# Hybrid encoder layer on one core: four places for the out projection's weight tiles, the residual stream loaded in pieces, and a quarter of the second half's new stream made by GpSimd

## The reference

```
xn   = rms_norm(h); P = xn @ w_in                    # q, k, v, gate_b, gate_c, conv_in
attn = stick-breaking attention over 8 heads         # exp(log_sigmoid(z) + reverse cumsum)
conv = gate_b * causal_conv3(gate_c * conv_in)
mix  = group_rms_norm(concat(attn, conv))
h    = h + rms_norm(mix @ w_out)                     # the out projection; "the new stream"
xf   = rms_norm(h)
ff   = silu(xf @ w_gate) * (xf @ w_up)               # 2048 -> 5632
h    = h + rms_norm(ff @ w_down)                     # 5632 -> 2048
```

## Time and profile before

| | us |
|---|---|
| median of 3 runs (2458.87 to 2461.89) | 2460.73 |
| the profiled execution | 2464.63 |
| its span | 2462.9 |
| TensorE busy | 2377.5 (97%) |
| VectorE busy | 1588.0 (64%) |
| ScalarE busy | 1052.2 (43%) |
| GpSimd busy | 95.9 (4%) |
| DMA, mean | 141 GB/s |

### The profile page before, as it was taken

The page is one execution under the profiler, slowest core; times in us unless marked ns, Lnnn a source line. Parts: engine busy times, 40 slices in busy tenths (PEclk is TensorE's granted clock), DMA queues, the critical chain, the costliest instruction groups (busy, mean ns, idle before and its releaser), DMA issues.

```text
span 2462.9 us, 42442 instructions
## 1 busy us (share of the span) xinstructions
PE 2377.5 (97%) x18250; PEld 2334.8 (95%) x18250; DVE 1588.0 (64%) x1852; ACT 1052.2 (43%) x1306; POOL 95.9 (4%) x158
## 2 busy tenths in 40 slices
PE   8999999999997988699999999999999989999998
PEld 7999999999997987599999999999999989999998
DVE  5323333343434556877877787777777778888886
ACT  6345444433233344444444444444444333333346
POOL 0000000000011111000000000000000000000002
PEclk9999999999998998899999999999999999999999
DMA  7222322232325565344444435344544766654562
GB/s 235 83 74 73 94 76 83 70 92 80 87 86 178 163 176 149 108 135 135 159 143 140 149 131 166 123 162 135 167 135 155 262 203 229 230 164 143 173 203 86
DMA packets 365406, 346.82 MB, mean 141 GB/s; under 512 B 9084, under 2 KB 323860, under 8 KB 365092
## 3 DMA queue, kind: packets, MB, share of 16 engines
q1 hardware_dynamic: 334528, 289.99, 37.8%
q10 hardware_dynamic: 30692, 54.12, 6.1%
HBM read 283.08 MB, written 61.00 MB: 140 GB/s over the span
## 4 chain that ended last, share of the span: by engine, by line
PE 84%; DMA 7%; DVE 5%; ACT 3%; issue 1%; SPq 0%; ACTq 0%; POOLq 0%; POOL 0%; DVEq 0%
PE ps L1033 36%; PE ps L449 23%; PE ps L1092 16%; DMA w_raw<-in_w_out_dram 5%; PE ps L750 4%; PE ps L694 2%; PE ps L949 2%; DVE w_lo L435 1%; ACT w_hi L429 1%; DMA ff_lo_scr<-hid_lo 1%; DMA panel<-in_w_down_dram 1%; DVE xs L1894 1%; DVE t_lo L1943 0%; DVE panel L1959 0%; PE ps L1014 0%
## 5 line engine op out<-in xcount | busy, mean ns | idle before, releaser
L1033 PE MATMUL ps<-xs,t_hi 128*128 128x272 f32 x4864 | 923.0, 289 | 23.6 <-DVE xs L1894 19.4
L1033 PEld LDWEIGHTS ps<-xs,t_hi 128*128 128x128 f32 x4864 | 766.3, 189 | 24.8 <-issue 24.8
L1033 PE MATMUL ps<-xs,t_lo 128*128 128x272 f32 x2432 | 704.8, 290 | 0.0
L1943 DVE TENSOR_TENSOR t_lo<-panel,t_hi 128x1024 fp32r<-128x1024 f32 (+1 forms) x402 | 482.0, 1199 | 221.9 <-ACT t_hi L1453 218.8
L1453 ACT CAST t_hi<-panel 128x1024 fp32r<-128x1024 f32 (+1 forms) x402 | 410.3, 1021 | 445.6 <-PE ps L1092 222.3
L1092 PE MATMUL ps<-xd,t_hi 128*128 128x272 f32 x2464 | 468.3, 289 | 9.9 <-DVE t_lo L1943 5.0
L1033 PEld LDWEIGHTS ps<-xs,t_lo 128*128 128x128 f32 x2432 | 458.6, 189 | 0.0
L1092 PEld LDWEIGHTS ps<-xd,t_hi 128*128 128x128 f32 x2464 | 388.6, 189 | 11.6 <-issue 6.3
L1092 PE MATMUL ps<-xd,t_lo 128*128 128x272 f32 x1232 | 357.1, 290 | 0.0
L435 DVE TENSOR_TENSOR w_lo<-w_raw,w_hi 128x1024 fp32r<-128x1024 f32 x162 | 198.1, 1224 | 239.8 <-ACT w_hi L429 239.6
L449 PE MATMUL ps<-act_hi,w_hi 128*128 128x280 f32 (+1 forms) x1536 | 328.8, 295 | 2.1 <-DVE act_lo L1719 1.9
(11 more groups left out here) (203 smaller groups left out, 2200.4 us busy)
## 6 DMA issues: line engine op xcount, KB each, us to landing
w_raw<-in_w_in_dram SPq DMA_DIRECT2D x96, 512.0 KB, 3.8
panel<-in_w_up_dram SPq DMA_DIRECT2D x44, 1024.0 KB, 5.4
panel<-in_w_gate_dram SPq DMA_DIRECT2D x43, 1024.0 KB, 5.1
w_raw<-in_w_out_dram SPq DMA_DIRECT2D x64, 512.0 KB, 4.0
panel<-in_w_down_dram SPq DMA_DIRECT2D x32, 1024.0 KB, 6.1
ff_hi_scr<-hid_hi SPq DMA_DIRECT2D x22, 952.0 KB, 4.5
ff_lo_scr<-hid_lo SPq DMA_DIRECT2D x22, 952.0 KB, 7.4
xd<-ff_hi_scr ACTq DMA_DIRECT2D x28, 544.0 KB, 7.8
```

What stands on the lines that cost most here:

```text
L1033: mm = nc.tensor.matmul(out, w[:, k, :], xs[x][:, part, k, :], start=begins and k == 0 and w is hi and part == 0, stop=k == KH - 1 and w i ...
L1943: V.tensor_tensor(tile_of(t_lo, i), raw_tile(i), tile_of(t_hi, i).bitcast(F32), ALU.subtract)\
```

## The change

It does five things.

1. From out tile 8 on (`WIDER`), tiles with k % 4 of 2 and 3 go to a second pair of places, `raw_more`, in the room of panel 0. Tile t from 12 on waits for tile t - 4 instead of t - 2. The first panel of step 0 now waits until all 68 tiles are subtracted, as the second did.
2. The stream is loaded in four pieces of four chunks, each behind one of the tile groups 2 to 5. VectorE waits for all four before its first addition, no longer before its first scaling.
3. In the last round (e = 31) neither ScalarE nor VectorE treats a tile; those tiles come behind it. The logarithm's table is loaded at the head of rounds 15 and 31, not between the roundings and the square.
4. Scaling and addition of the last four chunks of half 1 are GpSimd's. ScalarE waits for `pool_made` before it squares them. The combine T4 of step 0 and the split of the ring tiles T3 and T1 of step 0 stand ahead of the second row scale, no longer in step 0.
5. In step 46 (`LAST + 3`) the second panel is issued ahead of the wait for the last hidden activations and their stores, and five of the reloads of hidden activations come one step later.

```diff
+        raw_more = sb_at("raw_more", 121856, [P, 2 * TK * P])
+        WIDER = 8
+        def out_tile(phase, k):
+            return 4 * phase[1] + k if phase[0] == 4 else -1
-        def raw_slot(k):
+        def raw_slot(phase, k):
+            if out_tile(phase, k) >= WIDER and k % 4 >= 2:
+                return raw_more[:, (k % 2) * TK * P:(k % 2 + 1) * TK * P]
             return w_raw[:, (k % 2) * TK * P:(k % 2 + 1) * TK * P]
+        def raw_loaded(phase, k):
+            o = out_tile(phase, k)
+            if o >= WIDER:
+                in_place = (o - WIDER) // 4 + 1
+                if k % 4 >= 2:
+                    return out_loaded[k % 2], 16 * in_place
+                return w_loaded[k % 2], 16 * (loads_of((4, WIDER // 4, T_OUT), k % 2 - 2) + in_place)
+            return w_loaded[k % 2], 16 * loads_of(phase, k)
...
@@ load, on SP
-                if not known(t) or t >= 2:
+                o = out_tile(phase, k)
+                if o >= WIDER + 4:
+                    sp.wait_ge(lo_ready, t - 3)
+                elif o >= WIDER + 2:
+                    sp.wait_ge(n1_ready, HEADS + GROUPS)
+                elif not known(t) or t >= 2:
                     sp.wait_ge(lo_ready, t - 1)
...
-            sp.dma_start(resid, h_scr).then_inc(h_loaded, 16)
             for q in range(2, KC):
                 load_out(q)
+                if q < 6:
+                    c0 = 4 * (q - 2)
+                    sp.dma_start(resid[:, c0:c0 + 4, :], h_scr[:, c0:c0 + 4, :]).then_inc(h_loaded, 16)
...
-            sp.wait_ge(n1_ready, HEADS + GROUPS)
+            sp.wait_ge(lo_ready, T_FF)
             load_panel(0, 0)
-            sp.wait_ge(lo_ready, T_FF)
             load_panel(0, 1)
...
@@ the loop over steps, on SP
+                load_panel(step, 1)
                 if step == LAST + 3:
                     store_hidden(FF // 2 - 1)
-                load_panel(step, 1)
...
@@ square_stream, on ScalarE
-                act.wait_ge(h2_made, 4 * t + g + 1)
+                act.wait_ge(*((pool_made, 1) if (t, g) == (1, 3) else (h2_made, 4 * t + g + 1)))
@@ the out projection's rounds, on ScalarE (the same bounds on VectorE)
+                if n == KC - 1:
+                    load_log_table(1)
                 for half in range(2):
                     ahead = 2 * e + half + LEAD
-                    if 2 * e + half >= 2 and ahead < OUT_T:
+                    if 2 * e + half >= 2 and e < 2 * KC - 1:
                         round_weights((4, ahead // 4, T_OUT), ahead % 4)
...
-                if n == KC - 1:
-                    load_log_table(1)
...
-            for ahead in range(4 * KC + LEAD, OUT_T):
+            for ahead in range(4 * KC + LEAD - 2, OUT_T):
                 round_weights((4, ahead // 4, T_OUT), ahead % 4)
...
             load_log_table(2)
-            tile_high(ring(0, T2))
+            for q in (T2, T3, T1):
+                tile_high(ring(0, q))
             make_rstd(4)
...
@@ load_hidden_after
-                elif step == STEPS + 1 and 0 <= q < 5:
+                elif step == STEPS + 2 and 0 <= q < 5:
                     first = (7 + q,)
...
@@ VectorE
-                    dve.wait_ge(h_loaded, 16)
...
             def add_mix(t, g):
                 dve.wait_ge(scaled, 4 * t + g + 1)
+                dve.wait_ge(h_loaded, 16 * 4)
...
-            for g in range(-1, 4):
-                if g + 1 < 4:
+            for g in range(-1, 3):
+                if g + 1 < 3:
                     scale_mix(1, g + 1)
                 if g >= 0:
                     add_mix(1, g)
...
             combine(0, T3)
-            tile_rest(ring(0, T2))
+            combine(0, T4)
+            for q in (T2, T3, T1):
+                tile_rest(ring(0, q))
             dve.wait_ge(rstd_ready, 5)
...
@@ step 0 on VectorE: tile_rest of T3 and T1 and combine of T4 only "if step:"
@@ step 0 on ScalarE: tile_high of T3 and T1 only "if step:"
...
@@ GpSimd, behind the sums of the squares
+            h, mix_out = (x[:, KC - 4:KC, tokens_of(1)] for x in (resid, wide_c))
+            pool.wait_ge(rstd_ready, 4)
+            pool.wait_ge(out_copied, 2 * KC)
+            G.tensor_tensor(mix_out, mix_out, rstd[:, tokens_of(1)].unsqueeze(1).broadcast_to([P, 4, TH]), ALU.mult)\
+                .then_inc(pool_scaled, 1)
+            pool.wait_ge(pool_scaled, 1)
+            pool.wait_ge(h_loaded, 16 * 4)
+            G.tensor_tensor(h, h, mix_out, ALU.add).then_inc(pool_made, 1)
```

More of the change, by code:

```diff
@@ L277, in build_layer @@
         w_loaded = [sem(f"w_loaded{j}") for j in range(2)]
+        out_loaded = [sem(f"out_loaded{j}") for j in range(2)]
         hi_ready = sem("hi_ready")
@@ L332, in build_layer @@
         scaled = sem("scaled")
+        pool_scaled = sem("pool_scaled")
+        pool_made = sem("pool_made")
         h2_made = sem("h2_made")
@@ L434, in rest_of_weights @@
             engine.wait_ge(hi_ready, t + 1)
-            engine.tensor_tensor(w_lo[:, k % SLOTS, :], raw_slot(k),
+            engine.tensor_tensor(w_lo[:, k % SLOTS, :], raw_slot(phase, k),
                                  w_hi[:, k % SLOTS, :].bitcast(F32), ALU.subtract).then_inc(lo_ready, 1)
@@ L1523, in _ @@
                     finish_gate(step - 1, j)
-                tile_high(ring(step, T3))
+                if step:
+                    tile_high(ring(step, T3))
                 if step == 0:
@@ L1527, in _ @@
                 copy_out(m1, step, B11, "a", m1_copied)
-                tile_high(ring(step, T1))
+                if step:
+                    tile_high(ring(step, T1))
                 if step == 0:
@@ L2052, in _ @@
                 after_up = step % 2 == 0 and step > 0
-                tile_rest(ring(step, T3))
-                combine(step, T4)
+                if step:
+                    tile_rest(ring(step, T3))
+                    combine(step, T4)
                 if after_up:
@@ L2060, in _ @@
                     hidden_sums(step // 2 - 1)
-                tile_rest(ring(step, T1))
+                if step:
+                    tile_rest(ring(step, T1))
                 if step % 2 and step > 1:
```

8 lines of the change are left out of this document (4 added, 4 removed).

## The result

| | before | after |
|---|---|---|
| median of the runs shown beside each other (4 each), us | 2461.19 (2458.87 to 2461.89) | 2417.81 (2416.78 to 2419.07) |
| profiled execution, its span, us | 2464.63, 2462.9 | 2416.78, 2415.1 |
| TensorE busy | 2377.5 (97%) | 2357.7 (98%) |
| VectorE, GpSimd busy | 1588.0, 95.9 | 1590.3, 92.1 |

The ratio is 0.9826, 95% interval 0.9809 to 0.9843. The forecast was 2415.5 us, 2.3 us too low; the gain is 43.4 us where 45 were forecast.

A forecast was written before the change was run, and what follows sets the result against it. TensorE bounds nearly everything, except the load-bound out projection from 757 to 930 us. Savings of 33 + 2.5 (parts 2 to 4) + 9 = 45 us give 2419.6 profiled, about 2415.5 median; own range 2409 to 2422, overall 2406 to 2431.

The forecast's parts named there:

- Part 1: Out projection: four places and a stream in pieces remove waits and low clock; 33 us saved, bounds 22 and 36.
- the rival that the loads still bind: Out projection: ring slots not widened or pieces lasting over 3.9 us; ten us come back, 2426; chance 0.15.
- Part 2: End of the out projection: row scale 5.8 us after the last chunk instead of 10.3; 4.4 us saved.
- the table load comes before, the tiles are there: Behind the last out chunk: why the row scale comes 5.8 us after it, with 4.4 us saved.
- Part 3: New stream's second half: GpSimd and VectorE exclude each other, so normalization starts 5.4 us later after the row scale.
- the rival that they run side by side: New stream: GpSimd and VectorE work in parallel, second row scale 4.5 us earlier, 2411; chance 0.12.
- Part 4: Step 0: two subtractions and one combine (3.6 us) move ahead of the normalization; 3.5 us saved.
- Part 5: Down projection's start: earlier panel issue removes idles of 5.28 and 2.07 us and 2 of low clock; 9 saved.
- I cost it at nothing: Step 46: the moved pairs put 7.7 MB into 21 us, needing 19 us at 403 GB/s; no cost.
- the rival of a stall in steps 46 and 47: Down projection: the stall moves there as transfers exceed 42 us of products; nine us come back, 2425; chance 0.09.
- The median: Whole kernel: the profiled execution before is 3.9 us above its median, so 2419.6 profiled becomes about 2415.5.
- The slower side: Step 0 and after: TensorE stays at its lower clock, 700 slow matmuls give 2483; chance 0.02.

The follow-up runs named there:

- Experiment 2: The changed kernel with two places for the out projection's raw tiles again, the stream still in pieces: 2455.4 us.
- 3: The changed kernel with the stream loaded whole ahead of tile 8 again, four places kept: 2430.4 us.
- experiment 4: The changed kernel with TensorE's sum of the first half's folds issued one chunk later, behind chunk 25: 2417.0 us.
- experiment 10: The changed kernel with the last round's edit undone (tiles 65 and 66 treated in round 31, table loaded behind their roundings): 2419.0 us.
- Experiment 5: The changed kernel with VectorE making the whole new stream, while GpSimd does two same-size operations on unneeded data: 2421.7 us.
- experiment 1: The changed kernel with VectorE making all of the new stream, GpSimd none: 2413.4 us.
- experiment 12: The changed kernel with VectorE making the whole stream, the folds' sum one chunk later and the last round's edit undone: 2405.3 us.
- Experiment 9: The changed kernel with combine T4 and the splits and roundings of ring tiles T3 and T1 back in step 0: 2424.3 us.
- Experiment 11: The changed kernel with both down projection edits undone (stores ahead of step 46's second panel, five reload pairs a step earlier): 2429.4 us.
- experiment 7: The changed kernel with the five pairs of hidden reloads a step earlier again, step 46's panel still issued early: 2427.8 us.
- 8: The changed kernel with VectorE making the whole new stream and the folds' sum one chunk later: 2410.8 us.

## Why the prediction was right, step by step

**Part 1 (33 forecast, 34.1 measured).** The mechanism held: a load bound loop with two places, no wait above 0.6 us on the out tiles after 764 with four. Experiment 2 shows that the places carry it (27.5) and 3 that the pieces give 10.3. The wait before the folds was forecast at 3.9 and is 3.92; its price with the low clock, 5.3, is experiment 4's. Of the gain, 24.6 us are waits (34.8 before and 10.2 after in all of the stage, where 26.4 less were forecast), and the rest, 9.5, is mostly products at the lower clock, for which 7 were forecast. One reading behind it was wrong: a load was reckoned at 4.0 us and a piece at 3.9, but between 757 and 800 us they take 6.9 to 7.7 and 8.8 to land (medians). The condition of the rival that the loads still bind came true, its price didn't: the cover of some 13 us was enough.

**Part 2 (4.4 forecast, 4.9 measured): the sum was right, its cause wrong.** The prediction gave the gain to "the table load comes before, the tiles are there" as if both helped. Experiment 2 has the edit without the places, and the row scale comes 10.3 us after chunk, as before; experiment 10 has the places without the edit, and it comes after 3.5. So the places gave 6.8, and the edit took back 1.9, because it put two roundings behind the chunk that had fitted ahead of it.

**Part 3 (-5.4 forecast, -6.3 measured).** GpSimd got in exactly where it was expected, after the first and the second scaling; the first square came 8.3 us after the row scale (8.6 forecast). Experiment 5 separates the engines' exclusion from any dependence and gives it 4.6 us; the rival that they run side by side is out. The rest of the 6.3, 1.6 us, is low clock: the wait ahead of the sums is 3.1 us in experiment 1 too, where before it was 0.23, and in experiment 12, where the clock stays up, the stretch is 17.9 again.

**Part 4 (3.5, 3.4).** Experiment 9 shows it alone.

**Part 5 (9 forecast; 6.9 in the table, 8.5 for what was forecast, and 1.5 lost elsewhere).** The forecast was made of the waits 5.28 + 2.07 and 2 us of low clock at the start of the down projection. There, from the first down product on, 8.5 us went: 6.7 of waits and 1.8 of low clock, so the mechanism held and the low clock was sized well. Experiment 11 brings back the same 8.5. The waits gave less than 7.35 because the one of step 44 grew from 0.88 to 1.87: its panel, issued at 1902.89, lands after 14.62 us, with fourteen reloads of 544 KB beside it; before had as many there, so why it grew is open. What the prediction had at nothing is the 1.5 us behind step 0's last wait, where the granted clock is 0.72 in the changed kernel and was 1.00 before. It also named one delay, the late panel; experiment 7 shows a second, the store of the low parts, for which VectorE waits when the five pairs stand ahead. "I cost it at nothing" held for step 46's pairs; the rival of a stall in steps 46 and 47 is out, since the waits there are gone.

**The median.** The profiled execution of before was taken as 3.9 us above its median for no named reason. The windows at its end offer one: the low clock there, 4.7 us more than in the changed kernel's. Its other runs weren't profiled stretch by stretch, but their mean granted clock goes the same way: 0.987 in the run of 2457.6 us, 0.985 in the profiled one and in one of 2468.3. That subtracting the 3.9 was right was luck. The slower side, a low clock that persists through the feed-forward products, didn't come: after 18.31 us of idling the stretch to step 0 is 39.6 to 39.7 in all kernels with part 4, and the fall behind step 0's last wait costs 1.5 us and no more.

## What to carry to other kernels

When a stage is fed by a loop of load, conversion and next load whose period is close to the consumer's, more places are worth more than moving the one big transfer that shows up as the longest stall: here 27.5 us against 10.3. Before work is handed from VectorE to GpSimd, look for two-input operations of both at the same moment; here such a split cost 4.6 us, and undoing it was the best single step by medians. And once a change has removed a bottleneck, try its companion edits without each other: one that had been made for late tiles cost 1.9 us when the tiles were in time. Last, before a difference of a few microseconds between two profiles is put down to an edit, compare the granted clock in stretches that the edit doesn't touch: here a fall in one of them hid 1.5 of 8.5 us.

## What the runs showed of the hardware that I had not expected

- With a queue of two-input instructions on both sides, VectorE and GpSimd alternated one by one (1.2, 2.4, 1.2, 2.3, 1.2 us): VectorE did not keep GpSimd out by having its next instruction ready. This was so for dependent and for independent data (the changed kernel and experiment 5).
- A wait of 1.25 us left TensorE's granted clock at 1.00 in the seven microseconds behind it, one of 3.13 us at 0.52 (experiments 12 and 8). A wait of 2.43 us was followed by 0.60 in one execution and by 1.00 in another (the ends of before and of after), and the wait of 2.0 us in step 0 by 1.00 and by 0.72.
- Where TensorE had a wait for VectorE ahead of it, a fall of the clock cost nothing: 1.53 us less of waiting stood against 14 matmuls fewer in six microseconds (experiments 8 and 4, at the start of the out projection).
- The difference at the end alone moves the time of identical instructions by up to 4.7 us, so that single profiles of two kernels differ by more than their medians (47.8 against 43.4).
